# Two transformer blocks on one core: another order of the weights' splits around the output projections, the second projection's gated sum in PSUM, and first scores issued ahead of the wait for the values

## The reference, cut to what matters

```python
# block 1, mixer: two branches, gated, projected
y_sb  = stick_breaking_attention(q, k, v)      @ w_sb_o
y_mla = latent_attention(qn, qr, kn, kr, v)    @ w_mla_o
out   = (sigmoid(gate_sb) * y_sb + sigmoid(gate_mla) * y_mla) @ w_out
# block 2, mixer: convolution and forgetting attention, gated, projected
conv_out = silu(layer_norm(conv(u_val * sigmoid(u_gate)))) @ w_conv_out
attn_out = forgetting_attention(q, k, v, f)                @ w_attn_out
x = x + g1 * ((sigmoid(gate_c) * conv_out + sigmoid(gate_a) * attn_out) @ w_out)
# block 2, feed forward: top 4 of 32 experts for each token
x = x + g2 * moe_ffn(h2)
```

## Time and profile before

| What | us |
|---|---|
| timed runs | median 1878.69 (1876.75 to 1884.53, 3 runs) |
| the profiled execution: its time | 1876.13 |
| its span, first to last instruction | 1874.4 |
| PE busy | 1807.2 (96% of the span) |
| DVE / ACT / POOL busy | 942.9 / 522.1 / 828.5 |
| chain that ended last, shares | PE 71%, DMA 14%, DVE 4%, ACT 4%, issue 4%, POOL 3% |
| first projection begins / `w1` begins | at 448.71 / at 479.60 |
| second projection begins / `w2` ends | at 867.16 / at 917.19 |
| experts' first large matmul / DMA becomes the chain | at 937.96 / at 1208.07 |
| one tile of 8 blocks on PE, 24 matmuls, full clock | 2.8 |
| one tile of 8 blocks at half clock | 5.1 |

### The profile page before, as it was taken

The page is one execution under the profiler, slowest core; times in us unless marked ns, Lnnn a source line. Parts: engine busy times, 40 slices in busy tenths (PEclk is TensorE's granted clock), DMA queues, the critical chain, the costliest instruction groups (busy, mean ns, idle before and its releaser), DMA issues.

```text
span 1874.4 us, 29787 instructions
## 1 busy us (share of the span) xinstructions
PE 1807.2 (96%) x11046; PEld 1138.1 (61%) x11047; DVE 942.9 (50%) x1476; ACT 522.1 (28%) x847; POOL 828.5 (44%) x481
## 2 busy tenths in 40 slices
PE   7999999998999999999999999999999999999997
PEld 7999896677899997888733333333333333333332
DVE  6776642345687574766553333343444434433334
ACT  5334443534544346346310110110110101110111
POOL 0000000000000014756377777777777777777774
PEclk9999999999999999999999999999999999999999
DMA  8777443112477562433889999999999999999995
GB/s 344 264 265 262 168 177 113 61 58 92 162 258 248 201 205 101 147 113 134 345 368 430 428 428 429 427 429 429 428 429 428 429 396 415 429 428 429 428 429 216
DMA packets 55726, 560.94 MB, mean 299 GB/s; under 512 B 6032, under 2 KB 8208, under 8 KB 14736
## 3 DMA queue, kind: packets, MB, share of 16 engines
q1 hardware_dynamic: 55520, 560.01, 74.3%
q10 hardware_dynamic: 144, 0.07, 0.0%
HBM read 559.00 MB, written 1.05 MB: 299 GB/s over the span
## 4 chain that ended last, share of the span: by engine, by line
PE 71%; DMA 14%; DVE 4%; ACT 4%; issue 4%; POOL 3%; POOLq 0%; SPq 0%; DVEq 0%; ACTq 0%
PE bank L1213 15%; DMA stage<-w_exp_in 14%; PE bank L670 12%; PE bank L672 11%; PE bank L671 11%; PE bank L1302 8%; POOL ring L1744 3%; PE bank L1225 2%; PE bank L1191 2%; PE bank L926 1%; PE bank L651 1%; DVE arena L1769 1%; ACT w_hi L1360 1%; PE bank L1203 1%; DVE w_lo L1789 1%
## 5 line engine op out<-in xcount | busy, mean ns | idle before, releaser
L1744 POOL COPY ring<-stage 128x2048 f32<-128x2048 f32 x372 | 693.7, 1894 | 251.5 <-DMA stage<-w_exp_in 100.7
L1213 PE MATMUL bank<-ring,arena 128*64 128x512 f32 x2112 | 475.4, 597 | 15.7 <-POOL ring L1744 15.1
L1724 POOL TENSOR_TENSOR w_lo<-ring,w_hi 128x512 fp32r<-128x512 f32 x104 | 134.5, 1327 | 773.4 <-ACT w_hi L1360 773.4
L670 PE MATMUL bank<-x_hi,w_hi 128*128 128x256 f32 (+1 forms) x1336 | 386.2, 289 | 9.0 <-DVE x_lo L1825 4.5
L672 PE MATMUL bank<-x_hi,w_lo 128*128 128x256 f32 (+1 forms) x1336 | 380.4, 285 | 0.0
L671 PE MATMUL bank<-x_lo,w_hi 128*128 128x256 f32 (+1 forms) x1336 | 380.1, 284 | 0.0
L1213 PEld LDWEIGHTS bank<-ring,arena 128*64 128x64 f32 x2112 | 142.6, 136 | 312.4 <-issue 231.9
L670 PEld LDWEIGHTS bank<-x_hi,w_hi 128*128 128x128 f32 x1336 | 253.5, 190 | 24.9 <-issue 15.9
L1789 DVE TENSOR_TENSOR w_lo<-ring,w_hi 128x2048 fp32r<-128x2048 f32 x92 | 210.7, 2290 | 102.9 <-ACT w_hi L1360 100.7
L672 PEld LDWEIGHTS bank<-x_hi,w_lo 128*128 128x128 f32 x1336 | 253.9, 190 | 0.0
L671 PEld LDWEIGHTS bank<-x_lo,w_hi 128*128 128x128 f32 x1336 | 253.0, 189 | 0.1
(11 more groups left out here) (339 smaller groups left out, 1975.7 us busy)
## 6 DMA issues: line engine op xcount, KB each, us to landing
stage<-w_exp_in SPq DMA_DIRECT2D x124, 2048.0 KB, 10.5
stage<-w_exp_out SPq DMA_DIRECT2D x62, 2048.0 KB, 10.6
ring<-stream SPq DMA_DIRECT2D x120, 1024.0 KB, 4.8
arena<-ada SPq DMA_DIRECT2D x48, 512.0 KB, 4.0
ring<-w_exp_in SPq DMA_DIRECT2D x8, 1024.0 KB, 8.4
ring<-w_exp_out SPq DMA_DIRECT2D x4, 1024.0 KB, 13.9
cst<-const_in SPq DMA_DIRECT2D x1, 1584.0 KB, 19.5
arena<-b_exp SPq DMA_DIRECT2D x3, 384.0 KB, 8.3
```

The lines of the kernel that those rows point to most:

```text
L670: begin = mm(out_, wh, xh, start=start, stop=False)
L1213: last = mm(bank[2 + gu][pr, :], xT[:, k % 4, k // 4, :], ring[:, k, c0:c0 + 512], start=False, stop=(k == KD - 1), tile_position=pos)
L1724: nc.gpsimd.tensor_tensor(w_lo[:, BUF[p], c:c + REST_COLS], ring[:, p % RING, c:c + REST_COLS], w_hi[:, BUF[p], c:c + REST_COLS].bitcast(f32),
L1744: nc.gpsimd.tensor_copy(ring[:, j, :], stage[:, 2 * PAIR_PLACE[j // 2 % 3] + j % 2, :]).then_inc(in_place, 1)
```

## The change

1. Mixer 1: PE waits for 4 instead of 7 evacuations ahead of `z(0)`, and for all 7 behind it, ahead of the first gate tile.
2. Mixer 1, first projection: ACT makes the upper part of `MIX1_OUT[1]` ahead of the table load and of all gates, then gates 0 to 3, the upper part of `MIX1_OUT[2]`, gates 4 to 7; the splits of `[3]` and `[4]` come ahead of `x_hi` of m = 3 and 5. DVE's lower parts come behind m = 0, 2, 4.
3. Mixer 2: the sigmoid table is loaded ahead of the eight shifts of `x_mix2` instead of behind them.
4. Mixer 2: the values' projection goes to banks 6 and 7; PE waits for its evacuation behind `scores_fa(0)` and `scores_fa(1)`.
5. Mixer 2, h = 7: `high_conv` comes directly behind the four sigmoids, ahead of the weight piece's upper part.
6. Mixer 2, second projection: the gated sum is made in PSUM (`o2_sum`, banks 6 and 7 in turn) instead of SBUF. ACT and DVE read it there for the upper and lower parts. The copy of `expert_col` out of bank 6 comes ahead of it.

```diff
+        o2_sum = [bank[6 + i][:, 0:SEQ] for i in range(2)]
...
-            pe.wait_ge(evac["ukv"], 7)
+            pe.wait_ge(evac["ukv"], 4)
...
             z(0)
+            pe.wait_ge(evac["ukv"], 7)
...
-            natural(cur, KD, [(bank[t][:, :], lambda k, t=t: split_x(k, t * P, t * P + P)) for t in range(2)],
+            natural(cur, KD, [(bank[6 + t][:, :], lambda k, t=t: split_x(k, t * P, t * P + P)) for t in range(2)],
...
-            pe.wait_ge(evac["v2"], 2)
...
                     scores_fa(h + 1)
+                if h == 0:
+                    pe.wait_ge(evac["v2"], 2)
                 gate_tile(2 * h, "gates2")
...
-            open_gates("gates", graw, range(0, 2))
             split_piece(MIX1_OUT[1])
-            open_gates("gates", graw, range(2, KD))
+            open_gates("gates", graw, range(0, 4))
+            split_piece(MIX1_OUT[2])
+            open_gates("gates", graw, range(4, KD))
             for m in range(KD):
-                if m % 2 == 0 and m:
-                    split_piece(MIX1_OUT[m // 2 + 1])
+                if m in (3, 5):
+                    split_piece(MIX1_OUT[m // 2 + 2])
...
+            use(ACT.Sigmoid)
             for m in range(KD):
                 act.wait_ge(x_split, AT[x_split]["n1"] + m + 1)
                 A(x_mix2[:, m, 0:SEQ], x_mix2[:, m, 0:SEQ], ACT.Identity, bias=mod[:, m:m + 1])\
                     .then_inc(x_whole, 1)
-            use(ACT.Sigmoid)
...
                         A(conv_s[:, m, :], cv[:, m, :], ACT.Sigmoid).then_inc(ln_sigmoid, 1)
+                    high_conv()
...
-                if h == HEADS - 1:
-                    high_conv()
...
-                A(x_hi[:, m, 0:SEQ], x_out2[:, m, :], ACT.Copy).then_inc(x_high, 1)
+                A(x_hi[:, m, 0:SEQ], o2_sum[m % 2], ACT.Copy).then_inc(x_high, 1)
...
-                if m in (1, 3, 5):
+                if m in (0, 2, 4):
                     rest(MIX1_OUT[2 + m // 2])
...
-            gated("o2", graw2, mt2, x_out2, lower("w2", x_out2, SEQ))
             dve.wait_ge(numbered, 1)
             link(V.tensor_copy(expert_col[0:E, :], bank[6][0:E, 0:1]))
+
+            def lower_o2(m):
+                dve.wait_ge(x_high, AT[x_split]["w2"] + m + 1)
+                tt(x_lo[:, m, 0:SEQ], o2_sum[m % 2], x_hi[:, m, 0:SEQ].bitcast(f32), ALU.subtract).then_inc(x_split, 1)
+
+            for m in range(KD):
+                dve.wait_ge(proj, AT[proj]["o2"] + m + 1)
+                dve.wait_ge(gates_ready, KD + m + 1)
+                if m:
+                    dve.wait_ge(evac["o2"], m)
+                if m >= 2:
+                    dve.wait_ge(x_split, AT[x_split]["w2"] + m - 1)
+                b0 = 2 * (m % 2)
+                mark(tt(mt2[:, 0, :], bank[b0][:, 0:SEQ], graw2[:, m, :], ALU.mult))
+                mark(tt(o2_sum[m % 2], bank[b0 + 1][:, 0:SEQ], graw2[:, 8 + m, :], ALU.mult))
+                settle()
+                tt(o2_sum[m % 2], o2_sum[m % 2], mt2[:, 0, :], ALU.add).then_inc(evac["o2"], 1)
+                if m:
+                    lower_o2(m - 1)
+            lower_o2(KD - 1)
```

More of the change, by code:

```diff
@@ L355, in build @@
         mt2 = a.take(2, SEQ)
-        x_out2 = graw2[:, 0:8, :]
+        o2_sum = [bank[6 + i][:, 0:SEQ] for i in range(2)]
         sq_n2 = graw2[:, 8:16, :]
@@ L1619, in _ @@
             for t in range(2):
-                A(w2v[:, t, :], bank[t][:, :], ACT.Copy).then_inc(evac["v2"], 1)
+                A(w2v[:, t, :], bank[6 + t][:, :], ACT.Copy).then_inc(evac["v2"], 1)
             def exp_fa(h):
```

## The result

| What | kernel before | changed kernel |
|---|---|---|
| timed side by side, first time: median us | 1877.72 (1874.92 to 1884.53, 6 runs) | 1867.41 (1862.63 to 1870.39, 6 runs) |
| ratio, 95% interval | | 0.9924 (0.9900 to 0.9948) |
| timed side by side, second time: median us | 1882.87 (1878.12 to 1887.58, 11 runs) | 1867.20 (1864.02 to 1871.16, 6 runs) |
| ratio, 95% interval | | 0.9918 (0.9899 to 0.9936) |
| the profiled executions | 1876.13 | 1868.49 (span 1866.7) |

Faster by 0.8%, and the forecast of 1865.5 us is 1.9 us from the first median. The size is less certain. The ratio with its interval is not the quotient of the two medians above it: the medians differ by 10.3 us the first time and by 15.7 the second, the ratios stand for 14.3 (9.8 to 18.8) and 15.4 us (12.1 to 19.0). The profiled pair differs by only 7.6 us, where the sum said 12.1.

The account below looks back on a forecast made before the run. PE, busy 96% of the span, was taken as the bound. Gains of 12.1 us off 1876.13 gave 1864.0, or 1866.6 against the median 2.6 us higher; 1865.5 was taken between them, range 1859 to 1873.

Parts of the forecast that it names:

- the sum: Predicted gains of all parts added: 2.4 + 2.5 + 0 + 1.2 + 6.0 = 12.1 us.
- rival (c): Waits only change place: projection 1 gains nothing, clock drops behind z(1); gain 7.9 us or less, 1870 us; chance 0.18.
- The new wait: Projection 1, ahead of the fifth tile: PE waits 3.2 us for a gated sum, then loses 1.7 us of clock.
- the second piece of `w1`: It can't be split before x_hi of m = 7, and costs PE 0.5 us of wait.
- rival (b): Clock holds too, in mixer 2's scores and behind projection 1's 3.2 us wait: 2.9 or 1.7 us more, 1861; chance 0.22.
- the known wait: PE's wait of 1.2 us ahead of mixer 2's first scores, ending with ACT's two evacuations; predicted to go.
- the clock loss left in: Mixer 2's first scores: 3.4 us of lost clock expected to stay, since scores alone may lower the clock.
- The wait for the attention's last tile: Projection 2: PE's second half-tile waits 0.65 us for its lower part, made on DVE beside POOL.
- The stream: Experts' DMA loads wait for counts or places from earlier work, so they move equally; all 12.1 us counted.
- Rival (d): Experts' first DMA loads don't come earlier with PE; gain 0 to 5 us, 1876 us; chance 0.06.
- (e): Slower: POOL's pieces for projection 2 become the bound, from 7.3 us a piece; 1889 us at 9 us; chance 0.02.
- four stretches: Places behind PE waits, at 321, 457, 785 and 867 us, losing 1.7, 1.7, 3.4 and 1.7 us of clock.

Follow-up runs that it names:

- n_o1: Changed kernel with `x_hi` of m = 0 and 1 ahead of gates 4 to 7 in projection 1; median 1862.59 us, ratio 0.9882; repeated, 1861.74 us, 0.9887.
- n_fa: Changed kernel with mixer 2's first gate tile ahead of `scores_fa(1)`, not behind it; median 1865.02 us, ratio 0.9902.
- u_conv: Changed kernel with `high_conv` put back behind the weight's upper part and gate tile 14; median 1872.05 us, ratio 0.9930.
- a_o1: Kernel before with only the new order of splits and gates in projection 1; median 1881.72 us, ratio 0.9986.
- u_scores: Changed kernel with the first scores of both mixers waiting for the values again; median 1873.15 us, ratio 0.9948.
- n_mla: Changed kernel with only the latent attention's first half gate tile moved ahead of `scores_mla(0)`; median 1867.59 us, ratio 0.9915.
- again: The changed kernel timed once more, unedited; median 1867.20 us, ratio 0.9918 to the kernel before.

## Why the prediction was right

**Part 1.** 2.4 predicted, 2.3 measured in the pair. z(0) at 317.67, z(2) at 328.71. All executions with the part take 16.7 us there (16.69 to 16.73 in eleven), and in none does the clock fall behind z(1), which was rival (c)'s second half; the three without it take 18.97, 19.99 and 21.45. It is worth 2.3 to 4.8 us, and 2.3 was the least.

**Part 2.** 2.5 predicted, 2.8 in the pair. The new wait (3.2 predicted, 3.1), its place, and the second piece of `w1` (0.5 predicted, 0.3) are right, and n_o1 shows that its cause is. Behind the wait five of eight executions lose 1.7 us as predicted (51.0 to 51.3 us), n_fa loses 3.4 (52.37), and in two (u_conv, a_o1) the clock holds, which was rival (b)'s second half: 49.9 us. Holding is worth 1.1 to 1.3 us, not the 1.7 of lost clock; that a PE that comes later finds DVE further on would explain it, but isn't shown.

**Part 3.** Costed at nothing, and not tried alone. PE's time from the norm to mixer 2's first score is 278.3 to 278.4 us in the six executions with the part and no clock lost there; a_o1, without it, has 279.65, of which 1.2 is the known wait. So nothing is the right figure as far as one execution can show.

**Part 4.** 1.2 of wait predicted and gained, the clock loss left in, and it stayed: 3.4 us in every execution of the changed kernel's order. In the executions without the part it was 3.4 once and 5.1 twice. The reading that scores alone may lower the clock was right for two blocks in a row (n_fa).

**Parts 5 and 6.** 3.7 and 2.3 predicted; undone one by one they cost 3.4 and 2.5. Together 6.0 predicted, 6.2 in the pair. The wait for the attention's last tile is 0.57 (predicted 0.65).

**The stream.** The experts' transfers moved with PE: the mean rate between 860 and 900 us rose from 137 to 211 GB/s, and the first block comes 9.3 us earlier, and 9.7 earlier by the 32nd. Rival (d) is refuted, and so is (e): POOL's pieces became shorter. Rival (c) describes the profiled pair's total (7.6) by chance, and not by its mechanism.

**What was luck.** The terms and their mechanisms were right, but that the median came within 1.9 us of the forecast is in part luck: six runs of the changed kernel spread over 7.8 us, and the profiled one has 5.1 us more loss at the passage and 1.6 us more in the experts than the sum knows of. The prediction also took the clock for full but in four stretches; three more in the execution of before, 1.7 us each, were overlooked, and one of them is the passage.

**Where the size may be off.** The sum was 12.1; the ratios give 1877.72 x 0.0076 = 14.3 us and 1882.87 x 0.0082 = 15.4. Both intervals reach down to 12.1 and the first pair of medians gives 10.3, so the timings don't show that the sum was short. If it was, by two to three us, the profile shows a candidate: the sum was made against one execution of before in which three losses (z, scores, projection 2) were as small as in any. A second with all three, a_o1, pays 2.5 us more to z(2), 1.5 more in the first scores, and 4.0 more in projection 2. Over the 51 timed runs of the kernel before that stand beside the experiments, whose mean granted clock goes from 0.985 to 0.997, time and clock go together (correlation -0.92, 1.5 us for each 0.001), and the median clock is 0.989 against 0.993 and 0.994 for the changed kernel. The difference of 0.0045 at 1.5 us for each 0.001 is 6.8 us, an estimate. So nearly half of the gain in the timings goes with a fuller clock, 3.4 us of which the sum had counted (z(0) and projection 2). That the rest comes from the places listed is argued, from the executions without the parts (before, u_scores, a_o1, u_conv); it isn't shown run by run, since only one execution of each kernel has a trace (two of the changed kernel and of n_o1).

**Left open.** From the start of the experts' first block to that of the 32nd it takes 863.0 to 865.7 us in these kernels, with no order that I could see, and from the 32nd to the last 27.3 to 27.6 or 28.8 to 29.4 us, in kernels with and without the change (a_o1 29.07, n_fa 27.28). That is how an edit's gain can vanish: n_mla was 1.9 us ahead of **again** at the first block and 0.6 behind at the 32nd. Why DMA and the ring fall one way or the other wasn't settled.

## What to carry to other kernels

Follow each queue past the wait that you remove: the wait for the first gated sum moved two tiles on and kept its length, and one line more (the upper part ahead of gates that nobody needed yet) was worth as much as the whole reorder (3.5 against 2.8 us). A wait and a lost clock behind it are not a sum, since each can cover the other, so size a stage from several executions, and prefer stretches between fixed instructions to the total. Where VectorE works beside GpSimd, an operand in PSUM instead of SBUF gave 0.4 instead of 0.8 to 1.5 us, and made GpSimd's own work 8% shorter.

## What the runs showed of the hardware

- The granted clock falls with PE 100% busy and no wait anywhere near: 3.4 us lost in two score blocks in a row (products over 64 and over 8 partitions) in eight of eight executions, 0 in three of three with a tile of full matmuls between them. Up to 6.8 us were lost at the passage, where blocks of products with 64 columns of weights and score blocks stand close together; that these are the cause isn't shown.
- For one and the same order of work the loss differs by execution: 0, 1.7, 5.1 and 6.8 us at one place. The same wait of 3.1 us had a drop behind it in six executions and none in two. The trace of one execution tells what can be lost, not what is.
- The spread of the kernel's times, 20 us over 51 runs, goes with the mean granted clock (correlation -0.92).
- Beside GpSimd, a VectorE operation on 128 x 256 with both inputs in SBUF took 0.8 to 1.5 us, one with an input in PSUM 0.42 us, and GpSimd's piece 5.05 instead of 5.5 us.
